# Earlier turns in the state-space scan, and two key/value branches made with tokens on the output's partitions

## The chip, the cores and the metric

The kernel runs on one core of a Trainium2 chip. The metric is device time in microseconds (us) of one launch, the median of the runs. TensorE (PE in the profile; PEld is its weight load) does the matmuls, VectorE (DVE), ScalarE (ACT) and GpSimd (POOL) the rest, SyncE (SP) issues the weight transfers.

## The reference

Two residual layers on x (256 tokens x 2048), all float32, each a token mixer and a gated FFN:

```
layer 0: x += mamba2(rms_norm(x));  x += conv_ffn(rms_norm(x))
layer 1: x += nsa(rms_norm(x));     x += conv_ffn(rms_norm(x))

mamba2: z, xbc, dt = h @ w_in; xbc = silu(causal_conv(xbc)); 8 groups of 8 heads, chunks of 128 tokens:
  cum   = cumsum(dt * a);  decay = exp(where(causal, cum_i - cum_j, -inf))
  y     = (C B^T * decay * dt) @ x + (C @ state) * exp(cum);  state updated once, between the two chunks
  y     = (y + d * x) * silu(z);  y *= rsqrt(mean over the group of y^2) * norm_w;  out = y @ w_out
nsa: q, kc, vc, ks, vs, kw, vw, gates = h @ w_in       (16 query heads, 4 key/value groups of 128)
  compressed branch: kc, vc through a small MLP over windows of 32 tokens
  selected branch (ks, vs) and window branch (kw, vw): k = rms_norm(k) * k_norm, then softmax attention
  out = (sum of the three branches, each times its sigmoid gate) @ w_out
```

## The kernel before

Activations lie transposed: features on partitions, the 256 tokens along the free axis. Each float32 operand is a high part and a rest (`xn` holds both, side by side, 2 x 256 columns). A weight *unit* is 512 KB: 8 blocks of 128 x 128 in one of 4 ring slots. SP loads it into `raw`; ACT rounds it to `w_hi` (`round_unit`, L441) once TensorE has let go of the slot; DVE forms `w_lo` (`split_unit`, L1258); TensorE uses it (`gemm_unit`). While TensorE is at unit v of a phase, ACT and DVE prepare v + 4, and what else they do at step v is written by hand behind that (the tables `SCAN_PE`, `SCAN_ACT`, `SCAN_DVE`, the dictionaries `steps`). A block is two matmuls (L837, L838): weights stationary, tokens moving, the rest of the weights with 256 columns and the high part with 512. The sum over both halves of the bank needs ACT to copy one half (`take_cross`, L450) and DVE to add it (`tile_sum`, L1263), and in the phases that run on unnormalised activations another DVE multiplication by `rstd` (L1267).

Phase `ssm` has 8 bodies of 20 units, one for each group. Body g makes the group's x, B and C (units 0 to 11, with the convolution taps of `conv_tap_of`, L1366) and z (12 to 19), while the scan of group g - 1 runs between the units: `scan_turn` behind unit 0 (eight transposes L952, and B C^T, L953 and L954), `scan_xdt` at 1, `scan_ecum` and `scan_decay` (16 exponentials, L536) at 3 to 5, `scan_w` at 5, `scan_y` behind unit 9 (24 matmuls, L964 to L966), the squares at 11, `sum_squares` on POOL, `scan_sumsq` behind 14 (L971), `scan_norm` at 15, `scan_round` at 16, `scan_rest` at 17. The last group's scan runs in the first 16 units of `ssm_out`. POOL fetches the cumulative sums of the next group as soon as `scan_y` is done, multiplies x by d (L1821, waits for `scan_rest`) and then masks (L1825).

Phase `kvs` makes the keys and values of the selected and the window branch: 16 tiles of 2 units each, woven with 16 units of the compressor's matmuls (`cmp_unit`, L855 and L856; 4 blocks each with 2 matmuls of 256 columns). The keys come with features on partitions, so their norm is taken by TensorE: `key_sums` (L1029, four float32 matmuls of 512 columns on 32 output columns each), `turn_key_roots` (L1036), `key_scales` (L1044, four float32 matmuls of 512 columns that spread the roots), then DVE `norm_keys`. The values are needed with tokens on partitions: `turn_values` transposes them (L1052, 16 in all, four at the end of `kvs` and twelve in the first body of the next phase, `q`).

Of the kernel before, what the change touches and what calls it, by code (L numbers as in the profile page):

```python
# [27 lines left out]
P = 128  # L28
T = 256
L = 128  # L30
D_TILES = 2048 // P
RING = 4
# [19 lines left out]
FOLD_BANK = [2, 6]  # L52
# [12 lines left out]
PLAIN_TILES = 1  # L65

# [46 lines left out]
class Woven(Phase):  # L113
# [20 lines left out]
    def source(self, v):  # L134

        k, c = self.order[v]
        n = UNIT * P
        if k is None:
            part = slice(c % 8 * n // 2, (c % 8 + 1) * n // 2)
            return self.inner[c // 8 * 2:c // 8 * 2 + 2, :, part].rearrange("m p n -> p m n")  # L140
        return self.dram[self.tile_order[k], :, c * n:(c + 1) * n]


def trunk(nc, x_in, consts_in, head_in, w_ssm_in, w_ssm_out, w_gu0, w_gu1, w_down0, w_down1, w_nsa_in,
# [19 lines left out]
    with ctx:  # L164
# [58 lines left out]
        with ExitStack() as st:  # L223
# [15 lines left out]
            kqn = sb("kqn", [P, 1], F32, st)  # L239
            pr2 = sb("pr2", [P, 2, 2, 3 * L], F32, st)  # L240
# [9 lines left out]
            ksq = [q[:, 2 * n:2 * n + 2].rearrange("p a t -> p (a t)") for n in range(4)]  # L250
# [4 lines left out]
            kdiag = q[:, 0:8].rearrange("p a t -> p (a t)").rearrange("p (n k) -> p n k", k=L)  # L255
            keys = [kc[:, 0:2, NCMP:], kc[:, 2:4, NCMP:], kv[:, 16:18], kv[:, 18:20]]
# [72 lines left out]
        kdiag_ready, kbc_done = sem("kdiag_ready"), sem("kbc_done")  # L329
        ksq_ready, kss_done, kstd_ready, krs_ready, k_ready = sem("ksq_ready"), sem("kss_done"), sem("kstd_ready"), sem("krs_ready"), sem("k_ready")  # L330
        kqn_ready, vt_done, vt_ready = sem("kqn_ready"), sem("vt_done"), sem("vt_ready")
        gexp_ready, gsig_step, gt_done, gt_ready = sem("gexp_ready"), sem("gsig_step"), sem("gt_done"), sem("gt_ready")
        qsq_ready, qss_done, qstd_ready, rq_step = sem("qsq_ready"), sem("qss_done"), sem("qstd_ready"), sem("rq_step")
        kstd_turned, qstd_turned = sem("kstd_turned"), sem("qstd_turned")
# [23 lines left out]
        for name in ("gu0", "kvc", "gates", "kvs", "q", "gu1"):  # L358
            SCALED[ph[name].tile0] = n_scaled
            n_scaled += ph[name].tiles  # L360
        XN_READY = [4, 4 + D_TILES, 4 + 2 * D_TILES, 4 + 3 * D_TILES]

# [24 lines left out]
        def _(sp):  # L387
            def load(p):
                def body(i):
                    for v in range(p.body):  # L390
# [6 lines left out]
                        if p is ph["kvs"]:  # L397
                            dst = raw[:, slot] if p.order[v][0] is not None else raw[:, slot].rearrange("p (m n) -> p m n", m=2)
# [29 lines left out]
        def _(act):  # L428
# [23 lines left out]
            def stream_std(n):  # L452
                act.wait_ge(ssum_done, n + 1)
                total = ps[2][:, 0:T] if n else ps[2][:, T:2 * T]
                times = 1 if n else ROWS
                act.activation(rstd[:], total, ACT.Sqrt, scale=1.0 / (times * D_TILES * P), bias=eps[:, 0:1]).then_inc(std_ready, 1)
# [86 lines left out]
            def scan_std(g):  # L543
                act.wait_ge(gss_done, g + 1)
                act.activation(grs[:], ps[4][:, 0:T], ACT.Sqrt, scale=1.0 / (XT_G * P), bias=eps[:, 0:1]).then_inc(gstd_ready, 1)
# [5 lines left out]
            def ssm_body(g, nxt, scan=True):  # L551
                p = ph["ssm"]
                for v in range(p.body):
# [4 lines left out]
                    if v % 2 and v == DECAY_ENDS and scan:  # L558
                        scan_decay(g - 1, 2)
# [7 lines left out]
                    if scan:  # L567
                        for at, stage in SCAN_ACT:
                            if at == v:
                                stage(g - 1)  # L570
                    else:
                        dt_part(v)
                z_silu(g, 3)

            DECAY_ENDS = 5
            SCAN_ACT = ((1, scan_sbt), (3, scan_ecum), (3, lambda g: scan_decay(g, 0)), (4, lambda g: scan_decay(g, 1)),
                        (11, scan_square), (14, scan_std), (16, scan_round))
# [5 lines left out]
            def last_scan_step(v):  # L583

                for at, stage in ((1, scan_sbt), (2, scan_ecum), (2, lambda g: scan_decay(g, 0)), (2, lambda g: scan_decay(g, 1)),
# [82 lines left out]
            def key_square(n):  # L668

                act.wait_ge(cin_ready, 2)  # L670
                act.wait_ge(tile_out, ph["kvs"].tile0 + 2 * n + 2)
                act.activation(ksq[n].rearrange("p (a t) -> p a t", a=2), keys[n], ACT.Square).then_inc(ksq_ready, 1)

            def key_std():

                act.wait_ge(kss_done, 1)
                act.activation(ksq[0], ps[6][:], ACT.Sqrt, scale=1.0 / P, bias=eps[:, 0:1]).then_inc(kstd_ready, 1)
# [1279 lines left out]
```

## Time and profile before

| | |
|---|---|
| median of 3 runs | 2573.61 us (2572.65 to 2573.92) |
| profiled execution: time, and its span from first to last instruction | 2574.58 us, 2572.9 us |
| PE busy / PEld busy | 2566.3 us (100%) / 2253.1 us (88%) |
| DVE / ACT / POOL busy | 1790.5 us (70%) / 1415.8 us (55%) / 220.2 us (9%) |
| DMA, mean over the span | 187 GB/s |
| granted TensorE clock, mean | 1.000 of full speed (2.4 GHz) |

Busy is time in which an instruction of the engine ran, and the times of matmuls overlap in the records: what a matmul costs is read from the start of one to the start of the next. Times in timelines are counted from the span's start.

### The profile page before, as it was taken

The page shows a single profiled execution, that of the slowest core. Times are in us where ns is not written, and L with a number is a line of the kernel's source. Part 1 is how long each engine was busy: PE and PEld are TensorE (multiplying, and loading weights), DVE is VectorE, ACT ScalarE, POOL GpSimd, SP SyncE. Part 2 cuts the span into 40 slices and gives each one's busy share as a digit, 9 for nine tenths or more (in the row PEclk, how much of TensorE's full clock was granted, in tenths as well). Part 3 has the DMA queues.
Part 4 walks back from the last instruction along what each step waited for, and adds up shares of the span by engine and source line. Part 5 has one row for each costly group of instructions (what it writes and reads, how often), then busy time and mean ns, then how long its engine had stood idle before and what let it go on. Part 6 is the DMA issues. An engine that isn't in the chain of part 4 may idle for free.

```text
span 2572.9 us, 46087 instructions
## 1 busy us (share of the span) xinstructions
PE 2566.3 (100%) x15225; PEld 2253.1 (88%) x15225; DVE 1790.5 (70%) x2592; ACT 1415.8 (55%) x2182; POOL 220.2 (9%) x197
## 2 busy tenths in 40 slices
PE   9999999999999999999999999999999999999999
PEld 8888888888888888888888888888888888888888
DVE  8778777875677777775555686767777777775444
ACT  6676767754455555554444465675555555554333
POOL 0211122112100000000111000102200000000000
PEclk9999999999999999999999999999999999999999
DMA  6655555656555555556666675334555556556665
GB/s 213 230 198 193 196 198 197 201 179 189 179 196 191 190 189 187 190 191 185 189 190 192 193 234 200 116 98 140 186 190 189 188 186 194 188 188 187 189 191 169
DMA packets 139483, 481.59 MB, mean 187 GB/s; under 512 B 17329, under 2 KB 19441, under 8 KB 138384
## 3 DMA queue, kind: packets, MB, share of 16 engines
q1 hardware_dynamic: 136448, 467.20, 56.9%
q0 software_dynamic: 2368, 12.68, 1.4%
q8 instruction: 47, 0.77, 0.1%
q10 hardware_dynamic: 592, 0.71, 0.1%
q14 instruction: 28, 0.23, 0.0%
HBM read 478.28 MB, written 2.16 MB: 187 GB/s over the span
## 4 chain that ended last, share of the span: by engine, by line
PE 89%; DVE 5%; ACT 3%; issue 2%; DMA 1%; POOL 0%; ACTq 0%; DVEq 0%; SPq 0%; POOLq 0%
PE ps L838 48%; PE ps L837 25%; PE pq L838 5%; PE po L838 3%; PE pq L837 3%; DVE w_lo L1258 2%; PE po L837 1%; ACT w_hi L441 1%; DMA raw<-w_ssm_in 1%; PE po L1141 1%; DVE cv L1366 1%; ACT wcum L536 1%; PE pq L1127 0%; PE ps L897 0%; PE pq L855 0%
## 5 line engine op out<-in xcount | busy, mean ns | idle before, releaser
L1258 DVE TENSOR_TENSOR w_lo<-raw,w_hi 128x1024 fp32r<-128x1024 f32 (+1 forms) x896 | 1093.7, 1223 | 613.3 <-ACT w_hi L441 612.1
L441 ACT ACTIVATE w_hi<-raw 128x1024 fp32r<-128x1024 f32 (+1 forms) x896 | 933.3, 1043 | 797.6 <-PE ps L838 695.7
L838 PE MATMUL ps<-xn,w_hi 128*128 128x512 f32 x3904 | 1358.6, 391 | 0.0
L837 PE MATMUL ps<-xn,w_lo 128*128 128x256 f32 x3904 | 1098.5, 281 | 0.3 <-DVE gpad L1267 0.2
L838 PEld LDWEIGHTS ps<-xn,w_hi 128*128 128x128 f32 x3904 | 730.4, 187 | 159.0
L837 PEld LDWEIGHTS ps<-xn,w_lo 128*128 128x128 f32 x3904 | 737.8, 189 | 4.9 <-DVE w_lo L1258 1.9
L838 PE MATMUL ps<-hid,w_hi 128*128 128x512 f32 x1408 | 488.2, 391 | 0.0
L837 PE MATMUL ps<-hid,w_lo 128*128 128x256 f32 x1408 | 394.2, 280 | 0.0
L838 PEld LDWEIGHTS ps<-hid,w_hi 128*128 128x128 f32 x1408 | 263.3, 187 | 57.7
L837 PEld LDWEIGHTS ps<-hid,w_lo 128*128 128x128 f32 x1408 | 266.1, 189 | 0.0
L838 PE MATMUL pq<-xn,w_hi 128*128 128x512 f32 x528 | 184.3, 391 | 0.0
L837 PE MATMUL pq<-xn,w_lo 128*128 128x256 f32 x528 | 149.6, 283 | 0.1
L637 ACT ACTIVATE hid<-up 128x256 f32 (+1 forms) x88 | 36.7, 417 | 180.3 <-DVE up L1531 180.3
L838 PEld LDWEIGHTS pq<-xn,w_hi 128*128 128x128 f32 x528 | 98.8, 187 | 21.6
L838 PE MATMUL po<-xn,w_hi 128*128 128x512 f32 x304 | 106.6, 392 | 0.0
L450 ACT ACTIVATE cross<-ps 128x256 f32<-128x256 f32 x280 | 102.0, 364 | 0.0
L837 PEld LDWEIGHTS pq<-xn,w_lo 128*128 128x128 f32 x528 | 99.8, 189 | 0.7 <-DVE w_lo L1258 0.4
L1522 DVE SCALAR_TENSOR_TENSOR gcv<-gpad,cst,gcv 128x256 f32<-128x256 f32 x176 | 84.7, 481 | 13.2 <-DVE gcv L1522 13.1
L838 PE MATMUL pq<-y_ssm,w_hi 128*128 128x512 f32 x256 | 89.2, 392 | 0.0
L838 PE MATMUL ps<-o_nsa,w_hi 128*128 128x512 f32 x256 | 89.1, 391 | 0.0
L837 PE MATMUL po<-xn,w_lo 128*128 128x256 f32 x304 | 85.7, 282 | 0.0
L1534 DVE TENSOR_TENSOR hid<-up,hid 128x256 f32 (+1 forms) x88 | 37.4, 425 | 63.5 <-ACT hid L637 63.5
(299 smaller groups left out, 2444.8 us busy)
## 6 DMA issues: line engine op xcount, KB each, us to landing
raw<-w_gu SPq DMA_DIRECT2D x352, 512.0 KB, 3.9
raw<-w_ssm_in SPq DMA_DIRECT2D x158, 512.0 KB, 3.8
raw<-w_down SPq DMA_DIRECT2D x128, 448.0 KB, 3.4
raw<-w_nsa_in SPq DMA_DIRECT2D x82, 512.0 KB, 4.2
raw<-w_ssm_out SPq DMA_DIRECT2D x64, 512.0 KB, 3.7
raw<-w_down SPq DMA_DIRECT2D x64, 512.0 KB, 3.6
raw<-w_nsa_out SPq DMA_DIRECT2D x32, 512.0 KB, 4.3
wcum<-cum_scratch POOLq DMA_DIRECT2D x8, 1024.0 KB, 7.6
```

What stands on the lines that cost most here:

```text
L441: act.activation(w_hi[:, slot, 0:n * P], raw[:, slot, 0:n * P], ACT.Copy).then_inc(unit_rounded, 1)
L450: act.activation(cross[:, (p.tile0 + k) % 2, 0:n], bank(p, i, k)[:, n:2 * n], ACT.Copy).then_inc(cross_copied, 1)
L536: last = act.activation(wcum[:, h, c], wcum[:, h, c], ACT.Exp, bias=tk[:, 2 + c, bass.ds(g * GH + h, 1)])
L637: act.activation(hid[:, bass.ds(j, 1), 0:T], up[:].rearrange("p (o t) -> p o t", o=1), ACT.Copy).then_inc(hid_rounded, 1)
L837: pe.matmul(acc[:, n:2 * n], w_lo[:, slot, cols], x[:, kb, 0:n], start=(kb == 0), stop=False, skip_group_check=True)
L838: mm = pe.matmul(acc[:, 0:2 * n], w_hi[:, slot, cols], x[:, kb, 0:2 * n], start=False, stop=(kb == n_blocks - 1), skip_group_check=True)
L1141: pe.matmul(o[:, c], v_st[:, (2 * b + a) * P:(2 * b + a + 1) * P], pth[:, b, cut], start=(a + b == 0), stop=False)
L1258: TT(w_lo[:, slot, 0:n * P], raw[:, slot, 0:n * P], w_hi[:, slot, 0:n * P].bitcast(F32), ALU.subtract).then_inc(unit_split, 1)
L1366: STT(cv[:], xpad[:, j:j + T], cst[:, bass.ds(n * 4 + (CONST["ssm_conv_w"] + j), 1)], cv[:], ALU.mult, ALU.add).then_inc(conv_tap, 1)
L1522: STT(gcv[:], gpad[:, a:a + T], cst[:, bass.ds(j * 3 + (CONST["ffn_conv_w"] + 3 * l * FFN_TILES + a), 1)], gcv[:], ALU.mult, ALU.add).then ...
L1534: TT(row[:, T:2 * T], up[:], row[:, 0:T].bitcast(F32), ALU.subtract).then_inc(hid_ready, 1)
```

## The change

In `ssm`, `scan_turn`, `scan_sbt` and `scan_xdt` of group g move into body g itself (behind unit 16, at 17 and 17), the decays from units 3 to 5 to units 0 to 2 of the next body and `scan_w` to 3 (one body, that of group 1, keeps them at 3 to 5), `scan_sumsq` from 14 to 16 (into another bank), the norm from 15 to 18, its rounding from 16 to 19, and `scan_rest` from 17 to unit 0 of the body after. POOL masks before it multiplies by d.

In `kvs`, the 32 tile units hold other weights: each has 2 of the 16 contraction blocks of 4 tiles (pieces of 1 KB per partition and tile, where it was one of 4 KB), and is used as the moving operand, with the tokens' 128 x 128 blocks stationary. A set of 4 tiles fills two banks, tokens on partitions. The cross copies, sums and multiplications by `rstd` of 16 tiles give way to four times two DVE multiplications by a column (`set_out`); the squares of the keys are summed by ACT (`key_squares`, 16 activations with an accumulator), the root is a column, DVE scales (`scale_keys`), and TensorE transposes the normed keys (`turn_keys`). `key_sums`, `turn_key_roots`, `key_scales` and `turn_values` are gone. The column of roots of the stream's norm takes two small matmuls more in `stream_norm`.

```diff
         if k is None:
             part = slice(c % 8 * n // 2, (c % 8 + 1) * n // 2)
             return self.inner[c // 8 * 2:c // 8 * 2 + 2, :, part].rearrange("m p n -> p m n")
-        return self.dram[self.tile_order[k], :, c * n:(c + 1) * n]
+        m, at = 9 + SET_TILES[k // 4], (k % 4 * 2 + c) * 2 * P
+        return self.dram[m:m + 4, :, at:at + 2 * P].rearrange("m p n -> p m n")
...
-            SCAN_ACT = ((1, scan_sbt), (3, scan_ecum), (3, lambda g: scan_decay(g, 0)), (4, lambda g: scan_decay(g, 1)),
-                        (11, scan_square), (14, scan_std), (16, scan_round))
+            SCAN_ACT = ((0, 1, scan_ecum), (0, 1, lambda g: scan_decay(g, 0)), (1, 1, lambda g: scan_decay(g, 1)),
+                        (2, 1, lambda g: scan_decay(g, 2)), (11, 1, scan_square), (17, 0, scan_sbt), (17, 1, scan_std),
+                        (19, 1, scan_round))
...
-            SCAN_PE = ((0, scan_turn), (9, scan_y), (14, scan_sumsq))
+            SCAN_PE = ((9, 1, scan_y), (16, 1, scan_sumsq), (16, 0, scan_turn))
...
-            SCAN_DVE = ((1, scan_xdt), (5, scan_w), (10, scan_yz), (15, scan_norm), (17, scan_rest))
+            SCAN_DVE = ((0, 2, scan_rest), (3, 1, scan_w), (10, 1, scan_yz), (17, 0, scan_xdt), (18, 1, scan_norm))
...
+            def key_squares(n):
+
+                act.wait_ge(cin_ready, 1)
+                act.wait_ge(ksq_ready, n)
+                act.wait_ge(tile_out, ph["kvs"].tile0 + 4 * n + 4)
+                for a in range(2 * KVG):
+                    last = act.activation(kt_sq[:, a * P:(a + 1) * P], kt[n][:, a * P:(a + 1) * P], ACT.Square, accum_out=krs[:, 2 * KVG * n + a:2 * KVG * n + a + 1])
+                last.then_inc(ksq_ready, 1)
...
             def stream_norm(n):
                 pe.wait_ge(ssq_step, D_TILES * n)
+                if n == 2:
+                    for t in range(2):
+                        pe.matmul(ps[2][:, T + 2 * t:T + 2 * t + 2], ssq[:, t * L:(t + 1) * L], ones[:, 0:2], start=True, stop=True)
                 pe.matmul(ps[2][:, 0:T], ones[:], ssq[:], start=True, stop=True).then_inc(ssum_done, 1)
...
+            def set_unit(p, v, k, c):
+
+                n, u, slot = k // 4, k % 4 * 2 + c, (p.unit0 + v) % RING
+                accs = [ps[a][:].rearrange("p (m n) -> p m n", m=4) for a in SET_BANKS[n]]
+                if u == 0 and n < 3:
+                    pe.wait_ge(tile_out, p.tile0 + (-1, 0, 4)[n])
+                elif u == 0:
+                    pe.wait_ge(k_ready, 2)
+                pe.wait_ge(unit_split, p.unit0 + v + 1)
+                for b in range(2):
+                    kb = 2 * u + b
+                    hi, lo = (w[:, slot].rearrange("p (m k n) -> p m k n", m=4, k=2)[:, :, b] for w in (w_hi, w_lo))
+                    for t, acc in enumerate(accs):
+                        x_hi, x_lo = (xn[:, kb, a + t * L:a + (t + 1) * L] for a in (0, T))
+                        pe.matmul(acc, x_hi, lo, start=(kb == 0), stop=False, skip_group_check=True)
+                        pe.matmul(acc, x_hi, hi, start=False, stop=False, skip_group_check=True)
+                        mm = pe.matmul(acc, x_lo, hi, start=False, stop=(kb == D_TILES - 1), skip_group_check=True)
+                mm.then_inc(unit_used, 1)
...
+            def turn_keys():
+
+                pe.wait_ge(kt_ready, 1)
+                for n in range(2):
+                    for t in range(2):
+                        for g in range(KVG):
+                            mm = pe.transpose(ps[TURN_BANKS[2 * n + t]][:, g * L:(g + 1) * L], kt[n][:, (t * KVG + g) * P:(t * KVG + g + 1) * P],
+                                              ident[:])
+                        mm.then_inc(k_turned, 1)
...
+            def set_out(n, v):
+
+                dve.wait_ge(unit_used, p.unit0 + v + 1)
+                for t in range(2):
+                    dst = kt[n].rearrange("p (t g n) -> p t g n", t=2, g=KVG)[:, t] if n < 2 else kvt[:, :, 2 * (n - 2) + t]
+                    TS(dst, ps[SET_BANKS[n][t]][:].rearrange("p (g n) -> p g n", g=KVG), rst[:, 2 * t:2 * t + 1], None,
+                       ALU.mult).then_inc(tile_out, 2)
```

## Rows read from the trace of the kernel before

**Rows 1.** Waits of PE and PEld: us in total, times, longest us

```profile
PE ps L964 <- DVE wcum L1386: 0.5, 1, 0.5
...
PEld po L971 <- POOL xdt L1810: 1.8, 5, 0.4
```

**Rows 2.** Windows: the `kvs` phase (us; busy and count by engine; clock; DMA share; GB/s)

```profile
1469.90:1581.60 111.70, 111.61 (x678) 97.20 (x677) 86.28 (x106) 65.75 (x79) 0.52 (x1) 1.00 0.68 221
```

**Rows 3.** The chain that ended last: start us, us, engine and line

```profile
323.09 0.87 PE ps L952 x8
...
1540.97 1.00 PE pq L1029 x8
1556.12 0.79 PE pq L1036 x8
1563.49 1.72 PE ps L1044 x4
1565.21 1.72 PE po L1044 x4
```

**Rows 4.** Timeline of PE in `ssm`: start us, us, instruction

```profile
285.67 0.28 PE L837 MATMUL ps<-xn,w_lo 128*128 128x256 f32 x1
285.79 0.39 PE L838 MATMUL ps<-xn,w_hi 128*128 128x512 f32 x1
286.02 0.28 PE L837 MATMUL ps<-xn,w_lo 128*128 128x256 f32 x1
```

**Rows 5.** Timeline of PE in a compressor unit of `kvs`

```profile
1542.11 0.28 PE L856 MATMUL pq<-w_lo,cin 128*120 128x256 f32 x1
1542.23 0.28 PE L855 MATMUL pq<-w_hi,cin 128*120 128x256 f32 x1
```

**Rows 6.** Timeline of PE around `scan_sumsq`

```profile
305.33 0.39 PE L838 MATMUL pq<-xn,w_hi 128*128 128x512 f32 x1
305.74 0.70 PE L971 MATMUL po<-xdt,ones 128*128 128x256 f32 x2
...
306.39 0.40 PE L838 MATMUL pq<-xn,w_hi 128*128 128x512 f32 x1
```

**Rows 7.** Timeline of ACT at step 3 of a body of `ssm`

```profile
274.98 1.28 ACT L527 ACT_TABLE_LOAD   x1
276.28 1.06 ACT L527 ACTIVATE cex<-cex 128x1024 f32<-128x1024 f32 x1
277.24 1.26 ACT L536 ACTIVATE wcum<-wcum,tk 128x128 f32<-128x128 f32 x4
278.41 1.04 ACT L441 ACTIVATE w_hi<-raw 128x1024 fp32r<-128x1024 f32 x1
```

**Rows 8.** Timeline of DVE: `scan_norm`, and `scan_xdt` up to the next split

```profile
252.08 1.75 DVE L1403 RECIPROCAL grs<-grs 128x256 f32<-128x256 f32 x1
...
255.56 0.42 DVE L1263 TENSOR_TENSOR sz<-pq,cross 128x256 f32<-128x256 f32 x1
...
269.61 1.28 DVE L1377 TENSOR_TENSOR xdt<-ps,tk 128x512 f32<-128x512 f32 x2
...
271.64 1.22 DVE L1258 TENSOR_TENSOR w_lo<-raw,w_hi 128x1024 fp32r<-128x1024 f32 x1
```

**Rows 9.** Timeline of DVE at step 5 of that body: the split for unit 9

```profile
282.69 1.23 DVE L1258 TENSOR_TENSOR w_lo<-raw,w_hi 128x1024 fp32r<-128x1024 f32 x1
```

**Rows 10.** Timeline of ACT in `kvs`: from a tile's end to the next rounding

```profile
1501.09 0.36 ACT L450 ACTIVATE cross<-ps 128x256 f32<-128x256 f32 x1
...
1502.06 2.17 ACT L441 ACTIVATE w_hi<-raw 128x1024 fp32r<-128x1024 f32 x2
```

**Rows 11.** Timeline of ACT: an exponential of 128 columns with an accumulator

```profile
1733.96 0.48 ACT L718 ACTIVATE pr<-pr,nm,rq 128x128 f32<-128x128 f32 x1
...
1734.43 0.59 ACT L718 ACTIVATE pr<-pr,nm,rq 128x256 f32<-128x256 f32 x1
```

**Rows 12.** DMA issues: transfer, count, KB each, median us from issue to landing

```profile
raw<-w_cmp SPq DMA_DIRECT2D x16, 512.0 KB, 4.6
```

More of the change, by code:

```diff
@@ L357, in trunk @@
         SCALED, n_scaled = {}, 0
-        for name in ("gu0", "kvc", "gates", "kvs", "q", "gu1"):
+        for name in ("gu0", "kvc", "gates", "q", "gu1"):
             SCALED[ph[name].tile0] = n_scaled
@@ L361, in trunk, with crosses @@
         XN_READY = [4, 4 + D_TILES, 4 + 2 * D_TILES, 4 + 3 * D_TILES]
+        def crosses(p):
+            return p.tile0 - PLAIN_TILES - (ph["kvs"].tiles if p.tile0 > ph["kvs"].tile0 else 0)
         def norm_weight(n, m):
@@ L702, in _ @@
                     cin_round(v // 4 - 1)
-                if v in p.ends(0):
-                    take_cross(p, 0, p.ends(0)[v])
-                    if p.ends(0)[v] in steps:
-                        steps[p.ends(0)[v]]()
+                if v in p.ends(0) and p.ends(0)[v] in steps:
+                    steps[p.ends(0)[v]]()
                 for i in range(2):
@@ L969, in scan_sumsq @@
             def scan_sumsq(g):
+                total = ps[4] if is_body(g, GROUPS - 1) else ps[5]
                 pe.wait_ge(sq_summed, g + 1)
-                pe.matmul(ps[4][:, 0:T], ones[:], xdt[:, 0, 0:T], start=True, stop=True).then_inc(gss_done, 1)
+                if not is_body(g, GROUPS - 1):
+                    pe.wait_ge(tile_out, ph["ssm"].tile0 + 7 + (g + 1) * ph["ssm"].per_body)
+                pe.matmul(total[:, 0:T], ones[:], xdt[:, 0, 0:T], start=True, stop=True).then_inc(gss_done, 1)
             p = ph["ssm"]
-            SCAN_PE = ((0, scan_turn), (9, scan_y), (14, scan_sumsq))
+            SCAN_PE = ((9, 1, scan_y), (16, 1, scan_sumsq), (16, 0, scan_turn))
             def ssm_body(g, scan=True):
                 for v in range(0 if scan else 4, p.body):
+                    if scan and v == 2:
+                        pe.wait_ge(gstd_ready, g - 1)
                     gemm_unit(p, g, v, xn)
-                    if scan:
-                        for at, stage in SCAN_PE:
-                            if at == v:
-                                stage(g - 1)
-                    elif v == 15:
+                    for at, back, stage in SCAN_PE:
+                        if at == v and (scan or not back):
+                            stage(g - back)
+                    if not scan and v == 15:
                         turn_dt()
@@ L994, in _ @@
                 gemm_unit(p, 0, v, y_ssm)
-                for at, stage in ((0, scan_turn), (6, scan_y), (8, scan_sumsq)):
+                for at, stage in ((6, scan_y), (8, scan_sumsq)):
                     if at == v:
@@ L1055, in _ @@
+            def turn_keys():
+                pe.wait_ge(kt_ready, 1)
+                for n in range(2):
+                    for t in range(2):
[3 more added lines that the diff above has]
+                        mm.then_inc(k_turned, 1)
             p = ph["kvs"]
-            steps = {9: lambda: cmp_fold(0), 10: key_sums, 12: turn_key_roots, 13: key_scales}
+            steps = {9: lambda: cmp_fold(0), 10: turn_keys}
@@ L1425, in ssm_body @@
                         conv_pad(p, g, k)
-                    if scan:
-                        for at, stage in SCAN_DVE:
-                            if at == v:
-                                stage(g - 1)
+                    for at, back, stage in SCAN_DVE:
+                        if at + (FIRST_LATER - 1 if stage is scan_w and is_body(g, 1) else 0) == v and (not back or scan and (back == 1 or not is_body(g, 1))):
+                            stage(g - back)
                     if taps:
@@ L1446, in last_scan_step @@
             def last_scan_step(v):
-                for at, stage in ((1, scan_xdt), (6, scan_yz), (8, scan_norm), (9, scan_rest)):
+                if v == 0:
+                    scan_rest(GROUPS - 2)
+                for at, stage in ((6, scan_yz), (8, scan_norm), (9, scan_rest)):
                     if at == v:
@@ L1872, in _ @@
             pool.wait_ge(vcmp_moved, 16)
-            pool.wait_ge(vt_ready, 4)
+            pool.wait_ge(tile_out, ph["kvs"].tile0 + ph["kvs"].tiles)
             stage(0)
```

172 lines of the change are left out of this document (69 added, 103 removed).

## The prediction, made before the change was run

> **What bounds the kernel now.** I read the page first, then the waits of TensorE, the busy time by stage, the chain of work that ended last, and last the timelines of single steps. The page's table has PE busy for the whole span, at the full granted clock. In the waits of TensorE the reader should see how little there is: the longest group is 1.8 us in 5 waits, the sum of squares on POOL in front of L971 [rows 1]. So nothing that only makes ACT, DVE or POOL sooner can gain more than a few us; what counts is how many matmuls TensorE has to stream, and whether something newly makes it wait. Its rates: a 256-column matmul of the split weights starts 0.12 us before the next, one with 512 columns 0.23 us [rows 4], a pair 0.347 over eight pairs, so a tile unit is 8 x 0.347 = 2.77 us. In a compressor unit a 256-column matmul, with weights loaded for it alone, again takes 0.12 us [rows 5], eight of them 0.94 us. The cost goes with the columns; no row shows an exposed weight load.
>
> **The key/value phase.** It lasts 111.7 us [rows 2]. 32 x 2.77 + 16 x 0.94 = 103.8 us of that are units. The other 7.9 us are the steps on TensorE: key sums 1.00, roots 0.79, spreading the roots 1.72 + 1.72 [rows 3], the first four value transposes at 0.109 each (a group of eight takes 0.87 [rows 3]) 0.44, and 2.2 us of folds, changes between matmul kinds and short waits. All four named steps go: 5.7 us. The other twelve transposes, in the next phase, go too: 1.3 us. Removed: 7.0 us.
>
> Added: `turn_keys`, 16 transposes at 0.109 plus the change of kind, 1.8 us. Two small matmuls in the stream's norm; the small matmuls of L1036 take 0.1 us a record [rows 3] and a float32 matmul is two records, so 0.4 us.
>
> The tile units themselves: 12 matmuls of 512 columns in place of 8 pairs. Columns are the same (6144), the kind of moving operand is new. Nearest row: the compressor's matmuls, which also have weights moving, in two pieces of 128 columns, at the usual rate [rows 5]. So I take 0.230 for each, 2.76 us a unit, 0.4 us less over 32 units. Bounds: at the granted clock of 1.00 [rows 2], that is 2.4 GHz, 512 columns can't take less than 0.213 us, which would give 2.56 us a unit and 6.8 us less; and if a 512-column matmul needed two 256-column times (0.233) it would be 0.8 us more. I keep both ends.
>
> A rule here would say something else. The Trainium skill (TensorE: Matmul & The Clock Gate, section Back-to-back issue gap) gives N/2.4 + 2.5 ns, so 216 ns for 512 columns and 109 for 256; the pair in this trace takes 0.347, not 0.325. By that rule the units would give 32 x (2.77 - 12 x 0.216) = 5.7 us rather than 0.4, an estimate from the page; I go by the row.
>
> New waits in `kvs`. (a) The eight squares with an accumulator stand between two roundings at the ends of tiles 4 and 8. Nearest row: an activation of 128 columns with its accumulator read, 0.47 us from start to the next start [rows 11], so 3.8 us, where today the cross copy and one square take 1502.06 - 1501.09 = 0.97 [rows 10]. The rounding behind them is 2.8 us later, then its split, then TensorE. The splits around tile 4 are hardly ahead of TensorE today; those around tile 8 are 2 to 3 us ahead. DVE is relieved at the same time (per tile two instructions of 0.42 us, 32 in all, against eight larger). I take 0.9 us for the first place and nothing for the second; the ends are 0 and 5.6. (b) Set 3 waits for two banks that ACT empties behind its rounding at the end of tile 11: 1 + 2 x 0.5 us against two compressor units, 1.9 us: 0.3 us. (c) Transfers now have 512 pieces of 1 KB. The compressor's, with 256 pieces of 2 KB, land in 4.6 us [rows 12]; I take 5.4 for the new ones. A slot's round trip is then 5.4 + 1.0 + 1.1 = 7.5 us for four units, which TensorE takes 7.4 us for in the densest stretch and 8.7 on the average: covered, but with no reserve. Without that cover each us more of latency costs about 1 us at each dense stretch, up to 3. In return today's short waits (about 0.8 us, part of the 2.2) should go.
>
> Sum for this part: -7.0 + 1.8 + 0.4 - 0.4 + 1.2 - 0.8, and about 0.5 for changes of kind that go with the four steps: -5.3 us.
>
> **The scan.** Every matmul stays. `scan_sumsq` today takes from 305.33 to 306.39, 1.06 us; the two matmuls of the block beside it are 0.35 of this, its own two records about 0.43 [rows 6]. The remaining 0.28 is a short wait and the change of kind in and out. Behind unit 16 the wait is gone and the way out leads into float32 transposes: 0.2 us saved in 7 bodies, -1.4. The first scan's wait of 0.5 us for `scan_w` [rows 1] doesn't go: there the third part of the decays now stands behind the cross copy and a SiLU, with two more table loads of 1.28 us [rows 7], against 2 us that DVE saves on `scan_xdt` [rows 8]. Net +0.3.
>
> The new danger is in the six bodies after it. DVE has `scan_xdt` (2.0 us to the next split [rows 8]) and `scan_norm` (3.5 us [rows 8]) at steps 17 and 18 with three splits of 1.13 and two sums of 0.34. Then comes ACT's last SiLU, before it may round at step 0. From TensorE's end of unit 17: 1.05 (rounding) + 2.0 + 3.5 + 3 x 1.13 + 2 x 0.34 + 0.4 = 11.0 us, while TensorE is at the end of unit 0 after 3 x 2.77 = 8.3: ACT begins step 0 some 2.7 us late. Steps 0 to 2 cost it 3 x 0.95 for rounding, 1.3 + 0.96 for the table and `ecum`, 16 x 0.29 for the decays [rows 7], 0.8 for a copy and a convolution's start: 10.6 us. At step 3: rounding and split 2.2, DVE's sum 0.3, `scan_w` 2.3, the split for unit 8 1.2: 6.0. In all 2.7 + 10.6 + 6.0 = 19.3 us after the end of unit 0, and TensorE wants unit 8 seven units later, at 7 x 2.77 = 19.4. Today the split for unit 9 ends at 283.9 [rows 9], 1.7 us before TensorE begins that unit at 285.7 [rows 4]. So a reserve of 1.7 us shrinks to about none. I take 0.07 us a body, +0.4; each us more that this chain takes costs 6 us. Nothing else on TensorE waits for what moved: the squares are summed by POOL some 6 us before unit 16 ends.
>
> Sum: -1.4 + 0.3 + 0.4 = -0.7 us.
>
> **The whole.** -5.3 - 0.7 = -6.0 us. The profiled execution took 2574.58 us with a span of 2572.9 (1.7 around it); it becomes a span of 2566.9 and 2568.6 us. The median is 1.0 below the profiled execution, so the prediction is 2573.61 - 6.0 = 2567.6 us, 0.23% less. A change within 0.2% (5.1 us, down to 2568.5) counts as none, so this forecast lies at that edge.
>
> **The rivals.**
> *The long matmuls stream faster.* If what a pair takes above its columns' 0.320 us belongs to the 256-column matmul, the sets run at 0.213 and give 6.4 us more: 2561.2 us. For it: twelve weight loads rather than sixteen, always under a long matmul. Against: both matmuls of a pair show the surplus [rows 4]. The skill's formula for the gap, above, would come to nearly the same time: 5.3 us under the forecast, 2562.3, an estimate from that page.
> *The preparers give most of it back.* The chain in the scan is 0.4 us longer than I make it (2.4 us in six bodies) and squares and 1 KB pieces cost 1.5 us more: 2571.5 us, no change. For it: both margins are about nothing. Against: DVE loses work in `kvs`.
> *The scan's reserve breaks.* The chain is 2 us longer, for instance because the last SiLU before step 0 and its table wait for `scan_norm` and then hold the rounding: 6 x 1.9 = 11.4 us, 2579 us, slower than before. It decides above 1.9 us a body. For it: ACT is at 43 of 61 us in a body and the work is now bunched. Against: I have counted these instructions, at today's durations.
>
> **How the numbers follow.** Forecast 0.52 (of it 0.41 below 2568.5, 0.11 above), faster streaming 0.13, given back 0.29, broken reserve 0.06. Faster 0.54, same 0.40, slower 0.06. The range goes from 2561, the faster streaming, to 2573, which takes in the third case with the upper ends of (a) and (c). The forecast's own range is 2565 to 2570.
>
> **What would show it.** The `kvs` phase should last 107.3 us, from its first unit to the first of `q` (111.7 less 5.7, 0.4, 0.8 and 0.5, plus 1.8 and 1.2); a matmul of the sets start 0.230 us apart (right) or 0.213 (the first rival). The waits of TensorE should have no L971 any more, and at the splits for units 8 and 9 of bodies 2 to 7 waits of 0 to 0.3 us; 1 us or more there is the third rival. 1 KB transfers should land in 5 to 6 us, and ACT's eight squares take 3.8 us. The prediction fails most easily by one of two near-zero margins, since one of them counts six times.

## The result, and the profile after

The changed kernel takes 2579.47 us (median of 11 runs, 2578.7 to 2580.12), beside 2574.03 for the kernel before in the same comparison (11 runs, 2572.65 to 2575.2). The ratio is 1.0021, 95% interval 1.0013 to 1.003: 5.4 us slower, where 6.0 us faster was forecast. That is outside the forecast range. The profiled execution agrees: its span is 2578.4 us, 5.5 us longer than before, the granted clock 1.00. One run is left out of the ratios of this document: of the ten of `e6_old_order_on_pool` one took 3452 us at a granted clock of 0.68.

The waits of TensorE in the changed kernel (us in total, times, longest), where before [rows 1] the longest group had 1.8 us in 5 waits:

```profile
PE pq L848 <- DVE w_lo L1270: 5.7, 6, 1.1
PE ps L964 <- issue: 1.8, 1, 1.8
PE ps L848 <- DVE w_lo L1270: 1.7, 5, 0.4
...
PE ps L1057 <- ACT kc L698: 0.5, 1, 0.5
```

L848 is the first matmul of a block, L1270 the split of the weights. Six waits of 1 us and five of 0.4 belong to six bodies of `ssm`: one at unit 5 in each body, and one at unit 8, which in one body is too short to be listed. L964 is `scan_turn`, and its one wait is in the first body. By the start times of the units, beside those of before, the two places cost 1.3 and 0.65 us a body. The wait for the sum of squares (L971 in [rows 1]) is gone, as forecast.

The window of phase `kvs`, as in [rows 2], from its first matmul to the first of `q`:

```profile
1481.70:1588.02 106.32, 105.77 (x538) 89.67 (x536) 76.78 (x78) 65.63 (x96) 0.52 (x1) 1.00 0.73 232
```

It is 106.32 us long and was 111.70, 5.4 us less; 4.4 less was forecast for this window. So the key/value part did what was forecast and a little more, and the loss, about 12 us, is in the scan. One of the six bodies shows it. DVE, POOL and ACT at steps 0 to 2 of the same body that [rows 7] shows (start us, us, engine, line, and in brackets the idle time before it and what ended it):

```profile
272.23 1.22 DVE L1270 TENSOR_TENSOR w_lo<-raw,w_hi 128x1024 fp32r<-128x1024 f32 x1 [1.64 <-ACT w_hi L451]
273.37 1.22 DVE L1425 TENSOR_TENSOR y_ssm<-yz,y_ssm 128x1024 f32 x1
276.72 3.47 DVE L1270 TENSOR_TENSOR w_lo<-raw,w_hi 128x1024 fp32r<-128x1024 f32 x1 [2.13 <-ACT w_hi L451]
280.11 0.41 DVE L1275 TENSOR_TENSOR xpad<-ps,cross 128x256 f32<-128x256 f32 x1
...
274.86 1.89 POOL L1841 TENSOR_TENSOR yz<-xf,cst 128x1024 f32<-128x1024 f32 x1 [23.18 <-DVE y_ssm L1425]
276.71 2.40 POOL L1845 TENSOR_TENSOR cex<-cex,sbt 128x1024 f32<-128x1024 f32 x1
...
273.51 1.06 ACT L539 ACTIVATE cex<-cex 128x1024 f32<-128x1024 f32 x1
...
278.61 1.05 ACT L451 ACTIVATE w_hi<-raw 128x1024 fp32r<-128x1024 f32 x1
280.85 0.60 ACT L518 ACTIVATE cv<-xpad,cst 128x256 f32<-128x256 f32 x1 [1.19 <-DVE xpad L1275]
```

TensorE at unit 5 of the same body:

```profile
280.24 0.39 PE L848 MATMUL pq<-xn,w_lo 128*128 128x256 f32 x1 [1.04 <-DVE w_lo L1270]
```

The same split takes 1.22 us at 272.23 and 3.47 us at 276.72. It starts 0.01 us behind POOL's multiplication of exp(cum) into C^T's copy (L1845, 2.40 us, until 279.11) and ends 1.08 us after it, about its own length: by these times it did next to nothing until POOL's instruction was over. Two moves of the change put the two side by side. ACT's `scan_ecum` (L539) is through at 274.57, some steps sooner than before. POOL is then still at the multiplication by d (L1841), which now stands behind the mask and waits for `scan_rest` (L1425, moved to unit 0 of this body); it ends at 276.75, and only then does L1845 start. TensorE gets its unit at 280.24, just when the split ends. ACT loses another 1.19 us for the padded tile behind it. Before, the two hardly met:

```profile
277.42 2.41 POOL L1832 TENSOR_TENSOR cex<-cex,sbt 128x1024 f32<-128x1024 f32 x1 [10.40 <-ACT cex L527]
...
279.49 1.43 DVE L1258 TENSOR_TENSOR w_lo<-raw,w_hi 128x1024 fp32r<-128x1024 f32 x1 [3.50 <-ACT w_hi L441]
```

POOL ran while DVE idled for 3.50 us, waiting for ACT; the split behind it began 0.34 us before POOL ended, and was 0.2 us longer. The Trainium skill (SBUF — State Buffer, section SBUF: two separate sides) states that a DVE instruction with two inputs in SBUF and a GpSimd instruction that reads SBUF share one pair of ports as an exclusive lock: whichever starts first has it for its whole instruction, and the other blocks fully. By that rule the split would wait 2.39 us, until 279.11, and take 3.6 us; the trace has 3.47, so it agrees.

The prediction has no term for this. Four theories stood for the experiments. **Collision**: moving `scan_ecum` three steps forward, with `scan_rest` and the multiplication by d just before it, puts POOL's multiplication at the start of a split. **Chain**: the preparers' chain from the last SiLU to the split of unit 8 is longer than was counted. **First turn**: in the first body TensorE is at unit 16 before ACT has copied the turned step sizes. **Key/value part**: it costs something after all.

### The profile page after: what moved, and what is told of

Same layout as the page of the kernel before. It is cut to its first block and busy times, and to the rows that moved or that the text cites. A ratio compares the mean times of both kernels' runs of the same rounds, so it can differ in the third digit from the quotient of the medians.

```text
span 2578.4 us, 45780 instructions
## 1 busy us (share of the span) xinstructions
PE 2561.8 (99%) x15077; PEld 2244.8 (87%) x15077; DVE 1794.9 (70%) x2565; ACT 1417.0 (55%) x2196; POOL 208.9 (8%) x197
## 5 line engine op out<-in xcount | busy, mean ns | idle before, releaser
L1270 DVE TENSOR_TENSOR w_lo<-raw,w_hi 128x1024 fp32r<-128x1024 f32 (+1 forms) x896 | 1098.5, 1228 | 619.2 <-ACT w_hi L451 618.1
L849 PE MATMUL ps<-xn,w_hi 128*128 128x512 f32 x3648 | 1268.8, 392 | 0.0
L848 PE MATMUL ps<-xn,w_lo 128*128 128x256 f32 x3648 | 1027.3, 282 | 2.1 <-DVE w_lo L1270 1.7
L849 PEld LDWEIGHTS ps<-xn,w_hi 128*128 128x128 f32 x3648 | 682.9, 187 | 148.3
L848 PEld LDWEIGHTS ps<-xn,w_lo 128*128 128x128 f32 x3648 | 689.5, 189 | 8.1 <-DVE w_lo L1270 4.6
L848 PE MATMUL ps<-hid,w_lo 128*128 128x256 f32 x1408 | 394.6, 280 | 0.0
L848 PEld LDWEIGHTS ps<-hid,w_lo 128*128 128x128 f32 x1408 | 266.2, 189 | 0.0
L848 PE MATMUL pq<-xn,w_lo 128*128 128x256 f32 x528 | 149.8, 284 | 5.7 <-DVE w_lo L1270 5.7
L848 PEld LDWEIGHTS pq<-xn,w_lo 128*128 128x128 f32 x528 | 99.8, 189 | 8.1 <-DVE w_lo L1270 8.0
L460 ACT ACTIVATE cross<-ps 128x256 f32<-128x256 f32 x264 | 96.1, 364 | 0.0
L1380 DVE SCALAR_TENSOR_TENSOR cv<-xpad,cst,cv 128x256 f32<-128x256 f32 x144 | 81.7, 567 | 9.3 <-DVE cv L1380 1.4
L848 PE MATMUL po<-xn,w_lo 128*128 128x256 f32 x304 | 85.8, 282 | 0.0
```

The source lines that it names most:

```text
L460: act.activation(cross[:, (p.tile0 + k) % 2, 0:n], bank(p, i, k)[:, n:2 * n], ACT.Copy).then_inc(cross_copied, 1)
L848: pe.matmul(acc[:, n:2 * n], w_lo[:, slot, cols], x[:, kb, 0:n], start=(kb == 0), stop=False, skip_group_check=True)
L849: mm = pe.matmul(acc[:, 0:2 * n], w_hi[:, slot, cols], x[:, kb, 0:2 * n], start=False, stop=(kb == n_blocks - 1), skip_group_check=True)
L1270: TT(w_lo[:, slot, 0:n * P], raw[:, slot, 0:n * P], w_hi[:, slot, 0:n * P].bitcast(F32), ALU.subtract).then_inc(unit_split, 1)
L1380: STT(cv[:], xpad[:, j:j + T], cst[:, bass.ds(n * 4 + (CONST["ssm_conv_w"] + j), 1)], cv[:], ALU.mult, ALU.add).then_inc(conv_tap, 1)
```

## The experiments

Each kernel is timed beside the kernel before on the same chip, and the ratio is to that one, with its 95% interval, some 2.4 us to either side and more where there are few runs. The medians of the kernel before lie between 2573.79 and 2574.28 us in all these comparisons, so a difference between two medians below carries 0.5 us of doubt from that alone; what is said of 1 or 2 us rests on the traces beside it. "The changed kernel" is the one of the result.

**The two parts alone.** `e1_kvs_only` is the kernel before with the key/value part of the diff (sets, column roots, `turn_keys`), `e2_scan_only` the kernel before with the scan's tables. Of the edit of `e2` one table:

```diff
-            SCAN_PE = ((0, scan_turn), (9, scan_y), (14, scan_sumsq))
+            SCAN_PE = ((9, 1, scan_y), (16, 1, scan_sumsq), (16, 0, scan_turn))
...
```

> The kernel before with the key/value part of the change alone; the scan is as before. If the two parts are independent, the key/value part is worth what the traces of before and after show between the start of the stream's norm and the third phase of attention, 5.8 us: 2574.0 - 5.8 = 2568.2 us. The rival, that the 1 KB transfers or the new eviction cost something which the delayed scan hides in the changed kernel, gives 2570 us or more.

Measured: 2567.51 us (10 runs, before 2573.79), ratio 0.9976 [0.9966, 0.9985], so 6.3 us faster; span 2565.9.

> The kernel before with the scan part alone. If the whole loss is the scan's, 2574.0 + 11.2 = 2585.2 us, of which 2.0 us stand once, in front of the first scan_turn, and about 1.6 us in each of six bodies, at the splits for units 5 and 8. If a loss comes only from both parts together, 2576 us or less.

Measured: 2585.89 us (4 runs), ratio 1.0046 [1.003, 1.0063], 12.1 us slower; span 2584.8. Its waits are those of the changed kernel:

```profile
PE pq L836 <- DVE w_lo L1262: 5.8, 6, 1.1
PE ps L950 <- issue: 1.8, 1, 1.8
PE ps L836 <- DVE w_lo L1262: 1.4, 5, 0.4
```

-6.3 and +12.1 give +5.8, measured together +5.4: within the noise the two parts don't touch each other. The key/value part gains what it should, and the whole loss is in the scan.

**POOL's multiplication left out.** This kernel multiplies only 8 columns of one head, so the term of the carried state is left out of the result; everything else runs.

```diff
-                pool.tensor_tensor(cex[:], cex[:], sbt[:, L:2 * L].unsqueeze(1).broadcast_to([P, GH, L]), ALU.mult).then_inc(cex_ready, 1)
+                pool.tensor_tensor(cex[:, 0:1, 0:8], cex[:, 0:1, 0:8], sbt[:, L:L + 8].unsqueeze(1), ALU.mult).then_inc(cex_ready, 1)
```

> The changed kernel, in which POOL's multiplication of the state term (cex by C B^T, 1024 columns, 2.4 us) is cut to 8 columns, so the scan's state term is not the reference's; every semaphore and all else stays. Theory A: this multiplication now starts together with DVE's split of step 1 (3.47 us long instead of 1.22) and keeps DVE out; without it the split takes 1.2 us, the waits at units 5 and 8 shrink from 1.95 us a body to 0 to 0.7 us, and the time is 2568 to 2572.5 us. Theory B, the third rival of the prediction: ACT and DVE are late in any case because norm and xdt stand just before step 0; then the waits stay and the time is above 2577 us.

Measured: 2572.47 us (10 runs), ratio 0.9995 [0.9985, 1.0004], 7.0 us less than the changed kernel (7.2 by span). The split at step 1 is short again and the waits at unit 5 are gone, the others stay:

```profile
274.40 1.27 DVE L1270 TENSOR_TENSOR w_lo<-raw,w_hi 128x1024 fp32r<-128x1024 f32 x1 [2.13 <-ACT w_hi L451]
...
PE ps L848 <- DVE w_lo L1270: 1.8, 5, 0.4
PE ps L964 <- issue: 1.8, 1, 1.8
```

So the multiplication costs 7 us, and the wait at unit 8 has another cause.

**The same multiplication, all of it, in four instructions** of two heads each. Nothing is moved and nothing left out.

```diff
-                pool.tensor_tensor(cex[:], cex[:], sbt[:, L:2 * L].unsqueeze(1).broadcast_to([P, GH, L]), ALU.mult).then_inc(cex_ready, 1)
+                for k in range(4):
+                    last = pool.tensor_tensor(cex[:, 2 * k:2 * k + 2], cex[:, 2 * k:2 * k + 2], sbt[:, L:2 * L].unsqueeze(1).broadcast_to([P, 2, L]), ALU.mult)
+                last.then_inc(cex_ready, 1)
```

> The changed kernel, but POOL's multiplication by exp(cum) is made as four of two heads each (0.6 us each) in place of one of 2.4 us. If DVE is held only until the running POOL instruction ends, the split at step 1 takes 1.2 + 0.6 = 1.8 us at most in place of 3.5, the wait at unit 5 goes and the time is 2571 to 2573 us. If POOL keeps the port over all four, or takes it back before DVE gets through, the split stays at 3 us or more and the time at 2579.5 us.

Measured: 2572.37 us (10 runs), ratio 0.9994 [0.9984, 1.0003], 7.1 us less than the changed kernel (7.5 by span), as much as leaving the multiplication out.

```profile
273.99 1.80 DVE L1270 TENSOR_TENSOR w_lo<-raw,w_hi 128x1024 fp32r<-128x1024 f32 x1 [2.13 <-ACT w_hi L451]
...
273.97 4.82 POOL L1846 TENSOR_TENSOR cex<-cex,sbt 128x256 f32<-128x256 f32 x4
```

DVE waits for one piece, 0.6 us, then gets through; now POOL is held, and its four pieces take 4.82 us in all, which nobody waits for. This run separates the collision from every theory about the order on ACT, since the order is untouched. The length of one POOL instruction is what cost the 7 us.

**The collision put into the kernel before.** POOL waits for the second part of the decays, so that its multiplication starts near the work at steps 4 and 5.

```diff
                 pool.wait_ge(sbt_ready, g + 1)
+                pool.wait_ge(decay_ready, g * 3 + 2)
```

> The kernel before, with one thing more: POOL waits for the second part of the decays before its multiplication by exp(cum), so that the multiplication (2.4 us) starts about when the split at step 5 does. Theory (a DVE instruction with two float32 operands that starts together with a POOL multiplication is held until POOL's ends): that split goes from 1.2 us to about 2.5 or 3.5 us in the scan's bodies. Its reserve before unit 9 is 1.7 us, so TensorE waits 0 to 0.6 us a body: 2573.8 to 2577 us. Rival (the engines share their port piece by piece): the split takes 1.4 us at most and the time stays at 2573.8.

Measured: 2579.02 us (10 runs), ratio 1.0018 [1.0008, 1.0027], 5.1 us slower: the direction expected, with more than the 0 to 3 us expected.

```profile
284.11 2.41 POOL L1833 TENSOR_TENSOR cex<-cex,sbt 128x1024 f32<-128x1024 f32 x1 [14.78 <-ACT wcum L536]
...
281.81 1.22 DVE L1258 TENSOR_TENSOR w_lo<-raw,w_hi 128x1024 fp32r<-128x1024 f32 x1 [3.51 <-ACT w_hi L441]
282.95 3.85 DVE L1366 SCALAR_TENSOR_TENSOR cv<-xpad,cst,cv 128x256 f32<-128x256 f32 x3
286.72 1.21 DVE L1258 TENSOR_TENSOR w_lo<-raw,w_hi 128x1024 fp32r<-128x1024 f32 x1
```

POOL hit three convolution taps rather than the split: together 3.85 us, where three such take 1.74 elsewhere in this run. The split behind them came that much later, and the reserve of 1.7 us in front of unit 9 [rows 4, 9] was used up. By the start times of units, 1.6 us are lost in the first scanned body and 0.6 to 0.75 in each of the next five, there most of it at the sum of squares, which now comes later. (The first scanned body is a rough measure: `e1`, whose scan is that of the kernel before, takes 1.5 us less in it than the profiled run of the kernel before.)

```profile
PEld po L971 <- POOL xdt L1810: 3.9, 5, 0.9
```

This wait was 1.8 us before [rows 1]. The expectation had looked at the split alone.

**The multiplication later.** POOL waits for the third SiLU of the body in which it multiplies (not for the last group).

```diff
+                if late:
+                    pool.wait_ge(conv_act, g * 6 + 9)
                 pool.tensor_tensor(cex[:], cex[:], sbt[:, L:2 * L].unsqueeze(1).broadcast_to([P, GH, L]), ALU.mult).then_inc(cex_ready, 1)
...
```

> The changed kernel, in which POOL waits with the same multiplication for the SiLU of the third tile of the next body (step 7), for all groups but the last; nothing else differs. Theory A: the long split moves to the units that TensorE wants 4 us later, where it costs nothing, so about the time of the run before it, 2568 to 2573 us, unless scan_y now waits for the multiplication (up to 1 us a body, 6 us). Theory B: above 2577 us. If the 2.25 us that POOL takes from DVE cost the same wherever they stand, 2579 us.

Measured: 2609.94 us (4 runs), ratio 1.0137 [1.012, 1.0154]. Missed by far: the waits at unit 5 did go, but the third SiLU comes so late that `scan_y` waited for POOL.

```profile
PE ps L976 <- POOL cex L1847: 26.8, 7, 6.1
```

**The old order on POOL, and ACT relieved.** `scan_ecum` stands at step 16 of the group's own body, and POOL multiplies by exp(cum) first, by d second.

```diff
-            SCAN_ACT = ((0, 1, scan_ecum), (0, 1, lambda g: scan_decay(g, 0)), (1, 1, lambda g: scan_decay(g, 1)),
+            SCAN_ACT = ((0, 1, scan_ecum), (16, 0, scan_ecum), (0, 1, lambda g: scan_decay(g, 0)), (1, 1, lambda g: scan_decay(g, 1)),
...
+                        if stage is scan_ecum and (not is_body(g, 1) if back else is_body(g, 0)):
+                            continue
...
```

> The changed kernel, but from the second group on scan_ecum stands at step 16 of the group's own body, and POOL multiplies exp(cum) into C^T's copy before it multiplies x by d (for the first group as in the changed kernel). So the large multiplication on POOL runs when DVE has no split to start with it, and steps 0 to 2 of ACT lose a table load and an exponential (2.2 us) a body. Theory (the split at step 1 is held by POOL): the 1.3 us at unit 5 go in six bodies, and with ACT relieved the 0.65 at unit 8 as well, at the price of two more table loads at step 16: 2568 to 2571 us. Rival (the wait is only a chain that is too long on ACT, POOL has no part in it): ACT's relief gives the same, so this run alone does not tell the two apart, but the length of the split at step 1 does: 1.2 us by the first, whatever POOL does elsewhere; and the split that now starts beside the multiplication, if one does, takes over 2 us. If the rounding at step 16 is delayed by more than its reserve: above 2579 us.

Measured: 2570.84 us (10 runs), ratio 0.9988 [0.9978, 0.9997], 8.6 us less than the changed kernel. By the start times of units, what is left at unit 8 is 0.25 to 0.5 us a body. A collision remains, now with the shorter multiplication by d:

```profile
273.57 2.05 DVE L1272 TENSOR_TENSOR w_lo<-raw,w_hi 128x1024 fp32r<-128x1024 f32 x1 [1.19 <-ACT w_hi L451]
...
272.65 1.89 POOL L1844 TENSOR_TENSOR yz<-xf,cst 128x1024 f32<-128x1024 f32 x1 [11.23 <-DVE y_ssm L1427]
```

POOL ends at 274.54, the split at 275.62, 1.08 us behind it, as above. Beyond the 7.0 us of the collision this kernel gains 1.6 us more, from all its differences together: ACT has 2.2 us less to do at step 0, and a shorter collision remains.

**The first turn one unit later**, alone (`e5`) and with the edit of `e6` (`e7`).

```diff
-                        if at == v and (scan or not back):
+                        if at + (1 if stage is scan_turn and not scan else 0) == v and (scan or not back):
...
```

> The changed kernel, but in the first body alone scan_turn stands behind unit 17 and its scan_sbt and scan_xdt at step 18. Theory: the first scan_turn waits 1.8 us for tk_ready because ACT is some 4 us late in the first body and copies the turned step sizes only when TensorE already stands there; one unit (2.77 us) later that copy is done. So the wait of 1.8 us in one place goes and the kernel gains 1.8 us: 2577.6 us. Rival: ACT's and DVE's work at steps 17 and 18 of this body, now one step later, delays a split, and the wait comes back there: 2579.5 us.

Measured: 2578.39 us (10 runs), ratio 1.002 [1.001, 1.0029]; span 2576.4, 2.0 less than the changed kernel's; the medians differ by 1.1. `scan_turn` (L964) waits no more, but `scan_y` of this group now waits 0.9 us for `scan_w`.

> The changed kernel with both repairs tried before: scan_ecum at step 16 of the group's own body with POOL's large multiplication in front of the d times x one, and the first scan_turn behind unit 17. If the two waits are independent, their gains add up: 2570.8 less 1.1 to 2.0 us, 2569 to 2569.7 us. That would still be 1 to 2 us above the kernel with the key/value part alone (2567.5), since about 0.5 us a body at unit 8 stays.

Measured: 2570.87 us (11 runs), ratio 0.9987 [0.9978, 0.9996], no better than `e6`: `scan_y` of the first group waits 1.7 us where the turn had waited 1.8. The gains do not add. In this body the turn was not the only thing late.

**The decays back, the turns not.** `FIRST_LATER` holds for every body: `scan_ecum` is at step 3, the decays at 3 to 5 and `scan_w` at 5 again, everything else as in the changed kernel; `e11` has the first turn later as well.

```diff
-                        if at + (FIRST_LATER if at < 3 and is_body(g, 1) else 0) == v and (scan or not back):
+                        if at + (FIRST_LATER if at < 3 else 0) == v and (scan or not back):
...
```

> The changed kernel with the decays back at steps 3 to 5 and scan_w at 5 in every body; the turns, the sum of squares and the norm stay where the change put them. Theory: both waits of the six bodies belong to the decays at steps 0 to 2 (at unit 5 through POOL's multiplication, which then starts with a split, at unit 8 through the chain's length), so both go, 1.95 us in each of six bodies, 11.7 us, and the time is about that of the key/value part alone, less 0.3 us a body for the sum of squares beside the turn, plus 1.9 us for the first turn: 2567 to 2568 us. Rival: the norm at step 18 and scan_xdt at 17, which make ACT begin a body 3.2 us late, cause part of it wherever the decays stand: 2571 us or more.

> As the run before, and in the first body scan_turn behind unit 17 with scan_sbt and scan_xdt at step 18. If the first turn's wait is independent of the rest: 1 to 2 us less than the run before, 2565.5 to 2566.5 us, the fastest of all kernels here.

Measured: 2593.54 us (5 runs), ratio 1.0075 [1.0061, 1.0089], and 2597.18 (5 runs), ratio 1.0086 [1.0072, 1.01]. Both expectations missed. No wait at a split is left, so `scan_ecum` and the decays at steps 0 to 2 do make both; but this edit puts the last third of the decays behind a SiLU, with two table loads, and `scan_y` waits for it; the lower clock behind these waits, at the end of this document, makes up the rest and is why `e11` is the slower of the two:

```profile
PE ps L976 <- DVE wcum L1400: 17.2, 7, 3.0
```

The kernel before has that third in front of the SiLU. With that, and nothing else changed (`e12`; `e13` with the first turn later):

```diff
+                    if v == 5 and scan:
+                        scan_decay(g - 1, 2)
                     if v % 2:
                         if k or not is_body(g, 0):
                             take_cross(p, g, k)
...
```

> As e10 (decays back at steps 3 to 5 in every body), and the last third of the decays at step 5 stands in front of the cross copy and the SiLU, as in the kernel before, so no table has to be loaded twice for it. Theory (all of the six bodies' loss belongs to the decays at steps 0 to 2, and e10's new one to the two table loads at step 5): scan_y waits no more, and the time is that of the key/value part alone (2567.5), less 0.3 us in seven bodies for the sum of squares beside the turn, plus 1.9 us for the first turn: 2567.4 us. Rival: scan_y still waits for scan_w by 1 us or more, because ACT starts the body 3.2 us late: 2573 us or more.

> As e12, and in the first body scan_turn behind unit 17 with scan_sbt and scan_xdt at step 18. Theory: the first turn's wait of 1.9 us goes and nothing comes back: 2565.5 us, the fastest of all kernels here, 2 us below the key/value part alone. Rival (in the run with the decays sooner only 1.1 us of the 1.9 showed in the time): 2566.5 us.

Measured: 2569.6 us (11 runs, before 2574.28), ratio 0.9982 [0.9973, 0.9991], and 2567.08 (9 runs), ratio 0.9974 [0.9964, 0.9984]. The waits of `e12` are the first turn's and some that the other kernels have too:

```profile
PE ps L966 <- issue: 1.8, 1, 1.8
PE ps L912 <- POOL ones L1789: 1.1, 1, 1.1
```

POOL's multiplication is back where ACT's exponential releases it, near the end of DVE's idle time:

```profile
278.46 2.41 POOL L1847 TENSOR_TENSOR cex<-cex,sbt 128x1024 f32<-128x1024 f32 x1 [5.66 <-ACT cex L539]
```

The loss of the six bodies is then gone: `e12` is 9.9 us below the changed kernel, and differs from it in the place of `scan_ecum`, the decays and `scan_w` alone. The first turn is worth 2.5 us here; by the start times of the units 2.0 of them stand in the first body, and the rest isn't placed. `e13` beats both kernels; against the key/value part alone (0.9976) it is no better than the measurement can tell.

## Why the prediction was wrong, point by point

**The key/value part was right**, and about 1 us better than forecast: -5.3 forecast in all, -6.3 measured (`e1`). In the window of the phase -4.4 was forecast (107.3 us) and -5.4 measured (106.32). Its parts, first three matmuls of a set, then the squares of the keys with the read of the accumulator behind each:

```profile
1500.10 0.39 PE L1057 MATMUL po<-w_lo,xn 128*128 128x512 f32 x1
1500.32 0.39 PE L1058 MATMUL po<-w_hi,xn 128*128 128x512 f32 x1
1500.55 0.39 PE L1059 MATMUL po<-w_hi,xn 128*128 128x512 f32 x1
```

```profile
1512.28 0.29 ACT L684 ACTIVATE q<-kv 128x128 f32<-128x128 f32 x1
1512.48 0.19 ACT L684 ACTIVATION_READ_ACCUMULATOR q<-kv 128x1 f32 x1
1512.57 0.30 ACT L684 ACTIVATE q<-kv 128x128 f32<-128x128 f32 x1
```

The 512-column matmuls start 0.228 us apart over eight of them (forecast 0.230, first rival 0.213), which rules the faster streaming out, and the 0.216 of the formula that the prediction set beside it as well. Eight squares take 2.3 us, 0.29 each, not 3.8: the accumulator's read ends only after the next one has started, and the row taken for them [rows 11] held a longer exponential (0.48). No wait followed them, where 0.9 was priced. The wait for `k_ready` is 0.5 us (L1057 in the waits above; forecast 0.3). The transfers in 1 KB pieces landed sooner than forecast: median 4.5 us against 5.4, as those in 4 KB pieces did before in this phase.

```profile
raw<-w_nsa_in SPq DMA_DIRECT2D x34, 512.0 KB, 4.5
```

**The step that failed is the six bodies' chain**, priced at +0.4 and defended against the third rival with the words "I have counted these instructions, at today's durations". `scan_ecum` and the decays sooner cost 9.9 us (the changed kernel less `e12`). One duration was not today's: the split at step 1, 3.47 us in place of 1.22, because POOL's multiplication by exp(cum) moved forward with `scan_ecum` and, behind the multiplication by d, started with the split. That is 7.0 to 7.1 us (`e3`, `e9`), and the kernel before with a collision put in loses time too (`e8`, 5.1 us, against other DVE instructions). The prediction followed every instruction that moved on ACT, DVE and TensorE, and for POOL only the squares ("nothing else on TensorE waits for what moved"). It did not ask when POOL's two multiplications would now start, and against which DVE instruction. No run moves `scan_ecum` and leaves `scan_rest` where it was, so how much of the collision hangs on each of the two stays open.

**The other term of that chain was a little short.** From ACT's first rounding of the body to the end of the split for unit 8 it was put at 16.6 us. In the kernel without the multiplication, where nothing collides, it is 16.7:

```profile
268.81 1.06 ACT L451 ACTIVATE w_hi<-raw 128x1024 fp32r<-128x1024 f32 x1
...
284.32 1.22 DVE L1270 TENSOR_TENSOR w_lo<-raw,w_hi 128x1024 fp32r<-128x1024 f32 x1
...
268.38 0.28 PE L848 MATMUL po<-xn,w_lo 128*128 128x256 f32 x1
...
285.59 0.39 PE L848 MATMUL ps<-xn,w_lo 128*128 128x256 f32 x1 [0.41 <-DVE w_lo L1270]
```

TensorE starts unit 2 at 268.38, so it ended unit 0 at 265.6 and ACT was 3.2 us late, not 2.7. The prediction added up the lengths of instructions; the missing 0.5 us is mostly between them: in the same trace ACT's rounding starts at 257.49, 0.2 us after TensorE has ended unit 17. 3.2 + 16.7 is 19.9 us against the 19.4 that TensorE takes: 0.5 to 0.65 us a body, about 3 us, where 0.07 a body was forecast.

**The third rival came out by its number, and partly by luck.** A chain some 2 us longer in six bodies was its mechanism, and its price was 2579. The 9.9 us of the six bodies are near its 11.4. But the cause is not the one it named (a SiLU that waits for `scan_norm`), and the total fits because other misses nearly cancel: 1.5 us less than its 11.4 and 1 us more gained by the key/value part, against 2 us lost at the first turn.

**The first scanned group** was put at +0.3, for `scan_w`. That wait of 0.5 us [rows 1] went, but it is absent from `e1` too, whose scan is the old one, so its going says nothing of the change. In its place `scan_turn`, in the first body, waits 1.8 us for the copy of the turned step sizes, which ACT makes at its step 15, about 4 us late in this body:

```profile
67.83 0.42 ACT L510 ACTIVATE tk<-ps 128x320 f32<-128x320 f32 x1
...
68.35 1.07 PE L964 MATMUL ps<-ident,xf 128*128 128x128 f32 x8 [1.75 <-issue]
```

**The sum of squares beside the turn** was put at 0.2 us saved in each of 7 bodies. The start times of units in `e1` and `e13` give, in the middle bodies, 0.75 saved behind unit 14, 0.45 lost where the turn goes in behind 16 rather than 0, and 0.2 lost at `scan_y`: 0.1 us a body. In the bodies of groups 1, 2 and 7 it is nothing or less. The sign was right, the size at most half; what takes the 0.2 at `scan_y` stays open.

So the scan's +12.0 us (changed kernel less `e1`) is about 7 from the collision, 3 from the chain and 2 from the first turn, less what the sum of squares saves.

## What to carry to other kernels

When a step is moved, list also what it releases, on every engine, and ask which instruction of another engine each of those will now start beside. Here the dangerous ones were GpSimd's elementwise instructions of 1.9 to 2.4 us. Put such an instruction where DVE idles, or cut it into pieces shorter than the reserve of the DVE work near it; here four pieces gave back all that one had cost. And a chain counted with today's durations holds only for as long as no DVE and GpSimd instructions in it meet anew.

## What was not expected of the hardware

A wait of TensorE of some 3 us can cost more than itself. In `e11` (2597.18 us), the first matmul of a body's `scan_y`, and 5 us around it (the number behind POOL's is the granted clock):

```profile
301.27 0.69 PE L976 MATMUL ps<-wcum,xdt 128*64 128x128 f32 x2 [2.95 <-DVE wcum L1400]
...
300.00:305.00 5.00, 3.73 (x42) 3.74 (x44) 4.71 (x7) 3.72 (x6) 0.00 (x0) 0.66 0.23 75
305.00:310.00 5.00, 5.00 (x36) 4.33 (x33) 4.69 (x9) 3.65 (x6) 1.49 (x2) 1.00 0.68 225
```

TensorE stood still for 2.95 us, and over the 5 us in which the wait ended the granted clock averages 0.66, so for most of them the lower of its two levels (1.2 GHz) was granted; 5 us later it is at full speed again. In `e11` that happens at six of the seven such places, all but the first, where the wait is 1.8 us. From 100 to 520 us the clock averages 0.97, which by estimate costs 3% of 420 us, some 13 us; with the 18.6 us of waits that is the 31.0 us by which its span exceeds that of `e13`. It is not a fixed price: in `e10`, with six waits of 2.5 to 3.0 us, only three places show it. Two of them, the first behind a wait of 2.94 us, the second behind one of 2.92:

```profile
298.00:303.00 5.00, 3.98 (x54) 3.72 (x55) 4.71 (x7) 3.72 (x6) 0.20 (x1) 1.00 0.31 94
362.00:367.00 5.00, 3.95 (x43) 3.95 (x45) 4.71 (x7) 3.71 (x6) 0.00 (x0) 0.66 0.31 89
```

What decides between them is not shown. The waits of 1.0 us in the changed kernel lowered nothing; its clock is 1.00.

DVE and GpSimd also hold each other up in both directions: in `e9` it was GpSimd's four pieces that were stretched, to 4.82 us from the 2.40 of one instruction.
